# A second model's two layers: the first two weight tiles work on x before the norm's root is known, and the tile order changes

## What is computed

```python
for l in range(DEPTH):
    mod = c_act @ w_ada[l] + b_ada[l]
    shift, scale, gate = jnp.split(mod, 3, axis=-1)
    h = rms_norm(x, norm_g[l]) * (1.0 + scale[:, None]) + shift[:, None]
    proj = h @ w_in[l]
    gq, gk, gv, glr, gz, dq, dk, dv, dz = split_columns(proj)
    gqkv = jax.nn.silu(causal_depthwise_conv(jnp.concatenate([gq, gk, gv], axis=-1), conv_w[l]))
    ...
    o_gla = gla_branch(gq, gk, gv, glr, gz, w_gk[l], b_gk[l], gla_norm_g[l])   # ends in  * silu(gz)
    o_diff = diff_branch(dq, dk, dv, dz, qn_g[l], kn_g[l], lam, lam_init, diff_norm_g[l])
    y = jnp.concatenate([o_gla, o_diff], axis=-1).astype(x.dtype) @ w_out[l]
    x = x + gate[:, None] * y
```

## Time and profile before

| | |
|---|---|
| median of 3 runs | 1975.08 us (1974.81 to 1975.26) |
| profiled execution | 1969.22 us, span of the core 1967.4 us |
| granted TensorE clock over the span, mean | 0.982 |
| PE, PEld, DVE, ACT, POOL busy | 94%, 74%, 56%, 45%, 44% |

### The profile page before, as it was taken

How to read it: one execution, slowest core, us unless ns; L and a number is a source line. 1 busy time by engine, 2 the same in 40 slices (tenths; PEclk the granted TensorE clock), 3 DMA queues, 4 the chain that set the end, 5 groups by cost and what they waited for, 6 DMA issues and landing times.

```text
span 1967.4 us, 26718 instructions
## 1 busy us (share of the span) xinstructions
PE 1858.3 (94%) x8662; PEld 1453.7 (74%) x8662; DVE 1106.3 (56%) x1731; ACT 877.8 (45%) x1385; POOL 874.7 (44%) x1064
## 2 busy tenths in 40 slices
PE   7999989999999999999899999998999988999988
PEld 5666667887888788888788878886776656776756
DVE  5666647712762578677567217723675553675561
ACT  6667643412432355555434213323554533554441
POOL 3323246555766333334146555754443225443323
PEclk9999989999999999999999999998999989999999
DMA  4111124433442321112144334422212212222212
GB/s 151 60 60 53 54 58 152 160 92 113 153 138 96 96 65 60 59 54 64 54 139 164 103 107 136 154 95 85 75 65 65 65 43 86 64 75 59 70 44 75
DMA packets 49228, 175.32 MB, mean 89 GB/s; under 512 B 5472, under 2 KB 5600, under 8 KB 49136
## 3 DMA queue, kind: packets, MB, share of 16 engines
q1 hardware_dynamic: 42224, 148.98, 24.1%
q10 hardware_dynamic: 6912, 25.17, 3.7%
HBM read 172.03 MB, written 2.10 MB: 89 GB/s over the span
## 4 chain that ended last, share of the span: by engine, by line
PE 77%; DVE 10%; ACT 7%; issue 5%; POOL 1%; DMA 0%; DVEq 0%; ACTq 0%; SPq 0%; POOLq 0%
PE ps_g L233 22%; PE ps_g L237 21%; PE ps_g L240 21%; PE ps_zt L946 2%; PE ps_s L1436 1%; PE ps_o L1497 1%; ACT w_hi L205 1%; PE ps_o L494 1%; PE ps_o L974 1%; DVE scr L1610 1%; PE ps_zt L484 1%; PE ps_s L385 1%; DVE scr L1132 1%; PE ps_zt L476 1%; DVE scr L442 1%
## 5 line engine op out<-in xcount | busy, mean ns | idle before, releaser
L213 POOL TENSOR_TENSOR w_lo<-raw,w_hi 128x256 fp32r<-128x256 f32 x936 | 763.8, 847 | 903.7 <-ACT w_hi L205 903.1
L205 ACT ACTIVATE w_hi<-raw 128x1024 fp32r<-128x1024 f32 x274 | 288.9, 1055 | 381.4 <-PE ps_g L240 376.0
L233 PE MATMUL ps_g<-h_hi,w_hi 128*128 128x512 f32 x1424 | 411.2, 417 | 32.6 <-ACT h_hi L294 11.5
L237 PE MATMUL ps_g<-h_lo,w_hi 128*128 128x512 f32 x1424 | 376.1, 393 | 0.6 <-DVE h_lo L266 0.6
L240 PE MATMUL ps_g<-h_hi,w_lo 128*128 128x512 f32 x1424 | 373.7, 391 | 0.3 <-DVE w_lo L221 0.3
L233 PEld LDWEIGHTS ps_g<-h_hi,w_hi 128*128 128x128 f32 x1424 | 256.1, 191 | 116.0 <-issue 52.6
L237 PEld LDWEIGHTS ps_g<-h_lo,w_hi 128*128 128x128 f32 x1424 | 269.3, 189 | 61.8 <-DVE h_lo L266 1.9
L240 PEld LDWEIGHTS ps_g<-h_hi,w_lo 128*128 128x128 f32 x1424 | 268.9, 189 | 58.0 <-DVE w_lo L221 0.7
L233 PE MATMUL ps_g<-a_hi,w_hi 128*128 128x512 f32 x768 | 204.9, 403 | 16.3 <-DVE a_lo L1644 7.5
L237 PE MATMUL ps_g<-a_lo,w_hi 128*128 128x512 f32 x768 | 198.0, 394 | 0.0
L240 PE MATMUL ps_g<-a_hi,w_lo 128*128 128x512 f32 x768 | 197.1, 392 | 0.0
(11 more groups left out here) (169 smaller groups left out, 2051.7 us busy)
## 6 DMA issues: line engine op xcount, KB each, us to landing
raw<-weights SPq DMA_DIRECT2D x274, 512.0 KB, 3.5
scr<-ada_weights ACTq DMA_DIRECT2D x48, 512.0 KB, 4.4
x<-x_tiles SPq DMA_DIRECT2D x8, 256.0 KB, 5.4
y<-x SPq DMA_DIRECT2D x8, 256.0 KB, 3.2
lvmask<-level_masks SPq DMA_DIRECT2D x1, 512.0 KB, 7.9
mats<-squares SPq DMA_DIRECT2D x1, 448.0 KB, 6.5
vecs<-vectors SPq DMA_DIRECT2D x1, 95.5 KB, 2.0
wgk<-gate_weights SPq DMA_DIRECT2D x1, 32.0 KB, 8.2
```

The lines of the kernel that those rows point to most:

```text
L205: nc.scalar.activation(w_hi[:, t.rep % 2], raw[:, raw_slot(t)], ACT.Copy).then_inc(whi_ready, 1)
L213: ins = nc.gpsimd.tensor_tensor(w_lo[:, t.rep % 2, ks], raw[:, raw_slot(t), ks], w_hi[:, t.rep % 2, ks].bitcast(F32), ALU.subtract)
L233: nc.tensor.matmul(bank[:], w_hi[:, t.rep % 2, kk], rhs(k)[0], start=(first and n == 0), stop=False)
L237: nc.tensor.matmul(bank[:], w_hi[:, t.rep % 2, kk], rhs(k)[1], start=False, stop=False)
```

## The change

It does four things.

1. The tiles z0 and z1 of the first gla pair come first in a layer. They are multiplied not with h but with x times the norm's gain and (1 + scale), which is made while x is completed (`early_hi`, `early_lo` in the last phase of the MLP and of the output projection). The root is applied to their product where it leaves PSUM (`z_b`), and the shift's part of it, the product of the weights with the shift vector, comes from eight plain fp32 matmuls of one column for each tile (`shift_pe`) and is added as a bias in two ACT instructions (`zlog`).
2. The norm's matmul stands between the two halves of z0. h itself is made in the other pair of buffers (`h_buf`).
3. R and c0 follow, their first halves ahead of both second halves.
4. The first gla item has 8 halves in place of 12, with the silu steps of z0 and z1 hung into its list (`OWN["gla0"]`); the gate has a log-sigmoid buffer of its own.

```diff
-B2_COLUMNS = [GLA_R]
+B2_COLUMNS = [GLA_Z, GLA_Z + P, GLA_R]
...
+        def h_buf(n):
+            return (a_hi0, a_lo0) if n in (5, 6) else (h_hi, h_lo)
...
+        OWN["gla0"] = {i: list(OWN["gla"][i]) for i in OWN["gla"]}
+        for _i, _z in ((5, 0), (9, 1)):
+            for _k, _s in enumerate([("zlog", _z), ("zmin", _z), ("zexp", _z)]):
+                OWN["gla0"].setdefault(_i + _k, []).append(_s)
+            OWN["gla0"].setdefault(_i + 2, []).append(("evac3", 4 + _z))
...
-            steps = [("gemm", 0, 0), ("gemm", 0, 1), ("gate_in",)]
+            steps = [("start",), ("gate_in",)]
...
-                        due[1].insert(0, ("gate2", it[1]))
+                        due[2 if first else 1].insert(0, ("gate2", it[1]))
...
+        def shift_pe(pe, l, i):
+            t = At(T_B2 + l * B2_TILES + i)
+            pe.wait_ge(whi_ready, t.of(1, 1))
+            for k in range(KT):
+                ins = nc.tensor.matmul(ps_o[:, i:i + 1], raw[:, raw_slot(t), k], mod[:, l, k:k + 1], start=(k == 0),
+                                       stop=(k == KT - 1))
+            ins.then_inc(ws_done, 1)
+
+        def start_pe(pe, l):
+            T, n = T_B2 + l * B2_TILES, 5 + 2 * l
+            first = b2_rhs(n - 1)
+            shift_pe(pe, l, 0)
+            gemm(pe, At(T), T, first, H1, True, False, h_waits(n - 1), (x_ready, (6 + l) * KT - 1))
+            norm_pe(pe, 4 + l)
+            gemm(pe, At(T), T, first, H2, False, True, h_waits(n - 1))
+            shift_pe(pe, l, 1)
+            gemm(pe, At(T + 1), T + 1, first, ALL, True, True, None, (x_ready, (6 + l) * KT))
+            for half in (H1, H2):
+                for i in (2, 3):
+                    gemm(pe, At(T + i), T + i, b2_rhs(n), half, half is H1, half is H2, h_waits(n),
+                         reader(i - 2, l) if half is H1 else None)
...
+                elif s[0] == "zlog":
+                    n, u, ws = log_of(s, l), z_b[s[1]], ws_b[:, s[1]:s[1] + 1]
+                    act.wait_ge(z_out, 2 * l + s[1] + 1)
+                    act.wait_ge(ws_ready, 2 * l + 2)
+                    act.activation(g_ls.buf, u, ACT.Abs, bias=ws).then_inc(g_ls.abs_ready, 1)
+                    act.wait_ge(g_ls.abs_ready, n.v + 1)
+                    act.activation(u, u, ACT.Identity, bias=ws)
+                    g_ls.act(act, n)
...
+                        if k in (3, 6):
+                            i = k // 4
+                            dve.wait_ge(tile_used, T + i + 1)
+                            nc.vector.tensor_tensor(z_b[i], ps_g[(T + i) % 2][:], rstd_x, ALU.mult).then_inc(z_out, 1)
...
+                    for i in range(2):
+                        pool.wait_ge(ws_done, 2 * l + i + 1)
+                        split_lo(pool, At(T + i + 1))
```

More of the change, by code:

```diff
@@ L1318, in schedule @@
                 for half in range(n):
-                    steps.append(("gemm", FIRST_TILE[it] + half // 2, half % 2))
+                    if not first or half >= 2:
+                        steps.append(("gemm", FIRST_TILE[it] + half // 2, half % 2))
                     steps += due[half]
-                left = {i - n: due[i] for i in range(n, 16) if due[i]}
+                left = {i - n: due[i] for i in range(n, 20) if due[i]}
                 if it is None:
                     steps.append(("split",))
-                    for i in range(16):
+                    for i in range(20):
                         steps += due[i]
@@ L1334, in build_program @@
         SWISH = [s[1:] for s in STEPS if s[0] == "evac3"]
-        SILUS = [s if s[0] == "gate" else s[1:] for s in STEPS if s[0] == "gate" or s[1:] in SWISH and s[0] == "evac"]
+        SILUS = [s[1:] for s in STEPS if s[1:] in SWISH and s[0] == "evac"]
         def nth(order, key, l):
@@ L1380, in reader @@
         def reader(tile, l):
-            if tile == 0:
-                return glr_ready, l + 1
+            if tile < R_TILE:
+                return z_out, 2 * l + tile + 1
             if tile < FIRST_TILE["diff", 0]:
-                p, c = divmod(tile - 1, 6)
+                p = int(tile >= FIRST_TILE["gla", 1])
+                c = tile - FIRST_TILE["gla", p]
                 if c < 4:
@@ L1414, in b2_pe @@
                 it = s[-1]
-                if s[0] == "gemm":
+                if s[0] == "start":
+                    start_pe(pe, l)
+                elif s[0] == "gemm":
                     tile, half = s[1], s[2]
-                    gemm(pe, At(T + tile), T + tile, h_rhs, H2 if half else H1, not half, bool(half),
-                         h_waits(4 + l) if tile == 0 else None,
-                         reader(tile - 2, l) if tile >= 2 and not half else None)
+                    gemm(pe, At(T + tile), T + tile, b2_rhs(5 + 2 * l), H2 if half else H1, not half, bool(half), None,
+                         None if half else reader(tile - 2, l))
                 elif s[0] == "gate":
@@ L1723, in build_program @@
                 for name in ("ng00", "ng01", "ng10", "ng11")]
+        GAIN += [lambda d, l=l: mod[:, l, bass.ds(d + KT, 1)] if not isinstance(d, int) else mod[:, l, KT + d:KT + d + 1]
+                 for l in range(2)]
         @block.sync
```

162 lines of the change are left out of this document (102 added, 60 removed).

## The result

The changed kernel takes **1979.83 us** (median of 20 runs, 1975.91 to 1983.57) where the kernel before takes 1975.80 (20 runs, 1973.26 to 1978.36): a ratio of 1.0018, with a 95% interval of 1.0011 to 1.0025, so 2.2 to 4.9 us slower. The forecast was 1973.3, a small gain. The time is inside the range given, but the interval lies wholly above 1: the kernel is a little slower. The profile of the changed kernel is of the slowest of its 20 runs (1983.57), that of the kernel before (1969.22) of an execution faster than any of its 20, so the two profiles are compared stretch by stretch and not by their totals.

What follows compares the result with a forecast made beforehand. PE was 94% busy, with a nearly as long DVE and ACT chain beside it. 27.05 + 61.4 = 88.45 us to the read, before 90.2 and 88.45, gains 1.75 in the first layer: 1973.3 us, range 1966.5 to 1980.5.

Steps and rivals of the forecast that it cites:

- The step that failed: Layer start: R's split waits only for z0's tile, c0's for z1's; c0's w_lo costs PE about 0.25 us.
- the start: Layer's beginning to the end of c0: 26.8 us of PE work, 27.05 us in all.
- S: Zero point of the start's walk: the end of the last matmul ahead of the layer.
- E: End of c0, from which the conv stretch was counted; forecast at S+27.05.
- tight, but in time: Loop making h in the start: eight blocks end about S+21.2, PE wants block 7 at S+21.5.
- the four steps of z in the conv stretch: z0's and z1's minimum and silu, priced 0.7 us; if all four lose 0.55 a layer, 4.4 us worse, 1977.7.
- The sign of being wrong that I had named: A start of over 29 us, from the shift's price or the loop making h, would show the forecast wrong.
- The early hi and lo in the phase before: MLP's last phase and output projection: 0.7 us on ACT, 0.75 on DVE per block of x, put at nothing.
- The conv stretch: From E to the read behind the update: a DVE and ACT chain beside PE sets 61.4 us, before about 63.
- the 50.5 us of work: PE's own work between E and the read without z0 and z1, leaving PE standing about 11 us there.
- The clock's rival: Clock falls in the stall ahead of c2', 3.4 us later a layer, 1980.1 us; decides only beyond about 7 us; chance 0.12.
- Behind the read the orders are the same, so the gain is carried: After the read the engines' orders are unchanged, so the first layer's gain of 1.75 us lasts to the end.

Runs made afterwards that it cites:

- e3: The changed kernel with c0's w_lo handed over in two halves, PE's first low product waiting only for the first: 1975.84 us, ratio 0.9998.
- e9: The changed kernel with c0's w_lo made by DVE in one instruction instead of by POOL: 1974.42 us, ratio 0.9992.
- e8: The changed kernel with one of eight products in each shift, leaving the shift of z0 and z1 incomplete: 1978.65 us, ratio 1.0017.
- e12: The kernel before with ten idle products ahead of the second scores of the first attention head: 1970.76 us, ratio 0.9969.
- e4: The changed kernel with idle products in conv-stretch stalls: eight ahead of c0', five ahead of c2', four ahead of the read: 1977.51 us, ratio 1.0007.
- e6: The changed kernel with z0's and z1's steps moved ahead of c0 and c0's w_lo handed over by halves: 1969.83 us, ratio 0.9974.
- e2: The changed kernel with the steps of z0 and z1 moved from between the conv tiles to ahead of c0: 1970.53 us, ratio 0.9973.
- e7: e6 with idle products, twelve ahead of c2' and ten ahead of the first attention head's second scores: 1981.12 us, ratio 1.0028.

## Why the prediction was wrong

**The step that failed** is in the start: "R's own split waits only for z0's tile, c0's for z1's (S+15.9), whose w_lo costs PE about 0.25". What PE waits for c0's splits measured 0.62 + 1.75 = 2.4 us in each layer where 0.25 was allowed, so E came 2.2 us late a layer, 4.4 in all. With 4.4 added, 1973.3 becomes 1977.7. Two things had been sized wrong. POOL's w_lo and DVE's steps were taken at their undisturbed 2.8 and 0.75 us; side by side they are 4.14 and 1.10 to 1.2. From its start at 1384.12 a w_lo of 2.80 would have left PE some 0.4 of the 1.75 us. And ACT begins c0's w_hi at S+17.5 and not S+15.9, since it stands in ACT's order behind steps for h that wait for DVE; that is the 0.62 us, and most likely the 0.4. h itself was "tight, but in time", as said: PE never waits for it.

How firmly each part is shown: e3 takes the wait for w_lo alone away and gets 3.5 us. e9 takes w_lo from POOL, after which neither engine disturbs the other, the wait is gone, and S to the read is 88.5. As DVE also has w_lo done sooner than POOL could, the division of the 1.75 us into 1.34 of slowing and 0.4 of a late start is arithmetic from the rows and not an experiment. The 0.62 us is left in both; no run takes it away.

The Trainium skill ("SBUF — State Buffer", section "SBUF: two separate sides") has DVE with two SBUF inputs and GpSimd exclude each other. The trace agrees that each holds up the other (4.14 beside DVE's steps, 2.80 without them in e9). It doesn't show their whole recorded times kept apart: POOL's four and DVE's four steps would be 5.8 us one after another, and took 4.7 (1384.12 to 1388.80). I had weighed that against the four steps of z in the conv stretch, and not against the loop of h, where DVE works with two SBUF inputs without a pause.

**The start otherwise** was right: the shift (1.84 for 1.95), no wait ahead of the norm, full clock. The sign of being wrong that I had named, a start of over 29 us, came true, but not by the shift's price, and by the loop of h only in that ACT's split for c0 stands in it. And e8 says that the sum of PE's work was not what set E: with 3.2 us of it gone (14 of 16 passes, twice) E moved 0.1 to 1.3. The early hi and lo in the phase before, put at nothing, cost nothing that shows: S comes at 1360.0 to 1365.5 us in the thirteen profiles of the changed kernel and its variants and at 1360.6 to 1363.2 in the four of the kernel before (e12 with them), and the two latest (after and e4) had 27.2 us at the low clock ahead of S where most had 20.4. From the second read to the next S it is 177.1 us in e6 and in e12 alike, so they cost nothing ahead of the second layer either.

**The conv stretch** was right in its length (61.2 for 61.4), in the copies on ACT (that of c0' at E+34.0, forecast 33.5), in the places of PE's long stalls, and in its cause. e2 shows that cause: with z's steps off the chain it is 58.0. So taking away the two tiles' 10.9 us of PE shortened it by 1.8 (from 63.05), as forecast. Its figure for how long PE stands there was too high, 11 us for 6.1 and 6.65: the 50.5 us of work left out the gate's matmul, now behind E (1.12), and the 1.7 that a fall of the clock adds; the rest is not traced. It changed nothing in the sum, since the chain sets the length.

**The clock's rival** happened, with falls of 3.4 us, under the 7 us from which I had it decide; and in the stretch to the read it costs nothing, as said there (e4, one layer with a fall and one without; in after all six layers have one fall between E and the read).

**"Behind the read the orders are the same, so the gain is carried"** holds for the orders and not for the clock. From the first read on both kernels have the same stalls, and the clock falls there or not by execution. At the attention's stall it fell in 4 of 6 layers of before, in 5 of 6 of after, in 21 of all 26 profiled without products there (e7 left out, where PE waited 5.66 us and the clock fell in both layers), and in none of the six with them. From read to read the changed kernel has six falls in its six layers, one of them right behind the read in every first layer; before has three in six, none there. By the table, means of three profiles for both layers together: S to the read 180.9 in place of 178.6, read to read 73.2 in place of 71.4, the rest 361.0 in place of 360.4. That is 2.3, 1.8 and 0.6 us, 4.7 in all, beside 4.0 by the medians. The first is about what the 4.4 us by which E came late leave of a forecast gain of 1.75, and its cause is shown, by e3 and e9, but for the wait for w_hi. Of the second, about 0.6 is not the clock: read to read without a fall takes 35.2 us in after and 34.9 in before, a layer. The rest rests on three profiles of each kernel, so that the change makes the clock fall more often behind the read is a likely reading and no more. So some 2 us of the 6.5 between forecast and measured time stay without a shown cause.

## What to carry to other kernels

Where work is moved beside a loop that keeps DVE busy with two SBUF inputs, cost POOL's and DVE's instructions in each other's company (here 4.1 for 2.8 and 1.1 for 0.75) before calling a slack of 0.3 us "in time". When tiles leave a stretch that a chain of DVE and ACT sets, their element-wise steps must leave it too: moving the tiles, 10.9 us of PE, shortened it by 1.8, and placing their steps in the idle time ahead of it took off another 3 us a layer. Look for stalls of 2 to 3 us on PE even where they have always been: filling one with idle products gave 3 us in one kernel and 6 in the other.
